# A fused two-block transformer kernel: the second half of the first block spread over more gathers, sums of four gathered loads from the third tile on, norms and branches tile by tile, first gathers issued earlier

## What is computed

```python
# first block
x = x + concat([delta_rule(...) , multiscale_pool(...)]) @ w_out          # "front" work
x = x + _peer(_rmsnorm(x, norm_ffn_w), w_query, sub_keys, expert_down, expert_up)
x = _rmsnorm(x, norm_final_w)
# _peer: 8 heads x 16 experts for each token, out of 16384
q = xb @ w_query ; scores = q . sub_keys ; top_k(16) twice, then top_k(16) of 256 sums
act = gelu(einsum("td,thkd->thk", xb, expert_down[idx]))
out = einsum("thk,thkd->td", gate * act, expert_up[idx])
# second block (c_2, ada_w_2 give shifts, scales, gates)
h = modulate(rms_norm(x, g0), sh_m, sc_m);  y = stick_breaking_mixer(h, w_qkv, w_o)
x = x + gt_m * rms_norm(y, g1)
h = modulate(rms_norm(x, g2), sh_f, sc_f);  y = swiglu_ffn(h, w_in, w_out)
x = x + gt_f * rms_norm(y, g3)
```

## Time and profile before

| what | value |
|---|---|
| median of 3 runs (lowest, highest) | 2576.68 us (2569.09, 2582.97) |
| the profiled execution | 2573.54 us, span of its instructions 2571.7 us, mean granted clock 0.879 |
| busy in the span | PE 1975.4 us (77%), DVE 1311.2, POOL 959.4, ACT 859.8 |
| moved by DMA | 672.54 MB, of it 536.90 MB in the gather queue |
| front list ahead of the loop | up to about 255 us |
| gather loop, first dot to last | 261.4 to 1801.3 us |
| second block | from 1803 us on |

### The profile page before, as it was taken

One profiled execution on the slowest core, in us unless ns is written; L12 is line 12 of the kernel. 1 busy time (PEld: TensorE's weight loads), 2 busy tenths in 40 slices (PEclk: granted clock), 3 DMA queues, 4 the chain that ended last, 5 costly groups with the idle time before them and its releaser, 6 DMA issues.

```text
span 2571.7 us, 24837 instructions
## 1 busy us (share of the span) xinstructions
PE 1975.4 (77%) x8704; PEld 1153.5 (45%) x8704; DVE 1311.2 (51%) x2810; ACT 859.8 (33%) x2260; POOL 959.4 (37%) x725
## 2 busy tenths in 40 slices
PE   8897778878788868765556565555698996999996
PEld 7765555435334235311001110000487665888785
DVE  4523547677775554565667666765401542333301
ACT  3112233334343333333333333332423653222212
POOL 1200323356553333444454445544342002444342
PEclk9999888879799889888776787877799998999998
DMA  6112979989989899999999999999021001222221
GB/s 240 36 58 74 405 290 361 383 330 411 392 334 386 331 373 355 375 417 419 420 420 418 420 379 420 420 420 403 33 99 66 1 1 66 98 92 92 78 99 49
DMA packets 100668, 672.54 MB, mean 262 GB/s; under 512 B 11328, under 2 KB 11328, under 8 KB 31552
## 3 DMA queue, kind: packets, MB, share of 16 engines
q0 software_dynamic: 73728, 536.90, 51.7%
q1 hardware_dynamic: 26816, 134.06, 13.6%
HBM read 668.82 MB, written 2.10 MB: 261 GB/s over the span
## 4 chain that ended last, share of the span: by engine, by line
PE 56%; DMA 19%; DVE 8%; issue 6%; ACT 6%; POOL 5%; SPq 0%; DVEq 0%; POOLq 0%; ACTq 0%; PEldq 0%
PE ps L695 55%; DMA arena<-in_experts,arena_u 16%; POOL arena L1515 4%; DVE arena L1816 3%; DMA gtrow<-in_w_ada 1%; ACT arena L1310 1%; DMA arena<-in_w_ada 1%; ACT sel L1306 1%; ACT L1163 1%; PE ps L706 0%; DMA arena<-in_prow 0%; ACT arena L1169 0%; ACT arena L660 0%; ACT L1306 0%; DVE arena L1882 0%
## 5 line engine op out<-in xcount | busy, mean ns | idle before, releaser
L695 PE MATMUL ps<-arena 128*32 128x512 f32 (+4 forms) x4376 | 1125.3, 553 | 377.1 <-ACT arena L1310 362.7
L695 PEld LDWEIGHTS ps<-arena 128*128 128x128 f32 (+1 forms) x4376 | 493.1, 163 | 949.4 <-ACT arena L1310 539.8
L1515 POOL DMA_INDIRECT arena<-in_experts,arena_u x512 | 599.4, 1171 | 846.7 <-PE ps L695 757.5
L1816 DVE CUSTOM_DVE_ANT_0 arena<-arena 128x1024 f32<-128x1024 f32 x512 | 649.3, 1273 | 386.2 <-DMA arena<-in_experts,arena_u 374.6
L695 PE MATMUL ps<-r_low 128*128 128x512 f32 x1824 | 419.5, 392 | 9.7 <-DVE r_low L1844 7.6
L1538 POOL TENSOR_TENSOR r_low<-middle,r_low 128x1024 fp32r<-128x1024 f32 x98 | 235.6, 2404 | 512.7 <-ACT r_low L1349 512.7
L695 PEld LDWEIGHTS ps<-r_low 128*128 128x128 f32 x1824 | 343.3, 189 | 85.3 <-DVE r_low L1844 6.8
L1306 ACT ACTIVATE sel<-sel 128x1 f32<-128x1 f32 x512 | 102.3, 200 | 648.1 <-DVE sel L1816 647.2
L1349 ACT ACTIVATE r_low<-middle 128x1024 fp32r<-128x1024 f32 x98 | 103.6, 1058 | 281.4 <-PE ps L695 281.3
L1310 ACT ACTIVATE arena<-arena,sel 128x32 f32<-128x32 f32 x512 | 164.5, 321 | 17.2 <-ACT sel L1306 0.5
L695 PE MATMUL ps<-arena,consts 128*32 128x32 f32 (+2 forms) x544 | 75.0, 446 | 96.5 <-POOL arena L1498 69.4
(11 more groups left out here) (201 smaller groups left out, 1518.9 us busy)
## 6 DMA issues: line engine op xcount, KB each, us to landing
middle<-in_w_late SPq DMA_DIRECT2D x24, 2048.0 KB, 7.4
arena<-in_w_front SPq DMA_DIRECT2D x88, 512.0 KB, 7.7
gtrow<-in_w_ada SPq DMA_DIRECT2D x32, 512.0 KB, 8.3
arena<-in_experts,arena_u POOLq DMA_INDIRECT x512, 12.1
arena<-in_w_ada SPq DMA_DIRECT2D x16, 512.0 KB, 9.0
x<-in_x SPq DMA_DIRECT2D x4, 512.0 KB, 9.0
arena<-in_sub_keys SPq DMA_DIRECT2D x2, 1024.0 KB, 10.4
arena<-in_rows SPq DMA_DIRECT2D x4, 512.0 KB, 10.3
```

The costliest lines, as they stand in the source:

```text
L695: return nc.tensor.matmul(out_, lhsT, rhs, start=start, stop=stop_, skip_group_check=skip)
L1515: nc.gpsimd.indirect_dma_start(ring[n % RING], None, a["experts"], bass.IndirectOffsetOnAxis(ap=idxq[:, i % 4, k:k + 1], axis=0),).then_in ...
L1816: nc.vector.tensor_tensor_reduce(r[:, 0:D], r[:, 0:D], xrep[k % 4], 1.0, 0.0, ALU.mult, ALU.add, dots[:, n % 8:n % 8 + 1]).then_inc(s["dot ...
```

## The change

- **Pacing.** Beside the loop more loads are put between stages: projections `p` of half 1 with odd number 3 in place of 2, `u` of half 1 (six levels for each of two chunks) 3 in place of 2, queries `q` of half 1 4 in place of 2, queries 8 to 15 of half 0 3 in place of 2. By walking the two lists, the positions of half 1 are:

| stage | before | after |
|---|---|---|
| queries 8 to 15 of half 0 | 4 to 18 | 5 to 26 |
| n0, tr0 | 19, 22 | 27, 30 |
| p 0 to 11 | 25 to 57 | 33 to 71 |
| kt to i0 of chunk 2 | 70 to 75 | 84 to 89 |
| levels of chunk 2 | 77 to 99 | 91 to 119 |
| kt to i0 of chunk 3 | 113 to 118 | 133 to 138 |
| levels of chunk 3 | 120 to 142 | 140 to 167 |
| pz to om | 152 to 170 | 178 to 196 |
| wo to tr1 | 172 to 192 | 198 to 218 |
| q 0 to 15 | 193 to 224 | 219 to 278 |
| gp, gs (gates) | 228 to 277 | 282 to 331 |

- **Group.** From load 256 on `sums` takes four loads at a time; all four slots are freed together.
- **First loads.** POOL issues loads 0 to 7 right behind its stage `sel 0`, so ahead of the decode for head 1.
- **Tiles 0 to 2 in the loop.** Their final norm, second norm, transposes and modulated copies are done beside loads 337 to 345, 353 to 361 and 433 to 441. The scaling before the transpose is gone: PE multiplies x by a diagonal of the reciprocals (`tdiag`).
- **Seams.** Tile 3 alone is left for seam 1; ACT makes the `a_hi` copies in place of DVE; statistics, branches and the output DMA go tile by tile.

```diff
-        add("p", u, 2 if u else 3)
+        add("p", u, 3 if u == 0 or h == 1 and u % 2 == 1 else 2)
...
-                add("u", (c, lv), 2)
+                add("u", (c, lv), 2 + h)
...
-        add("q", j, 2)
+        add("q", j, 4 if h == 1 else 3 if j > 7 else 2)
...
+        def beside(n, lag):
+
+            gates = STAGES[-1][0]
+            return {gates + 6 + lag: 0, gates + 22 + lag: 1, gates + 102 + lag: 2}.get(n)
...
-            sp.wait_ge(s["fin"], T)
-            sp.dma_start(out.rearrange("b (t p) d -> p (b t) d", p=P), x[:, :, :]).then_inc(s["out"], 16)
+                sp.wait_ge(s["fin"], t + 1)
+                sp.dma_start(out.rearrange("b (t p) d -> p (b t) d", p=P)[:, t, :], x[:, t, :]).then_inc(s["out"], 16)
...
+            def group(n):
+
+                return GROUP if n < 2 * TOPK * PH else 2 * GROUP
...
-                    for k in range(n - GROUP + 1, n + 1):
+                    for k in range(n - group(n) + 1, n + 1):
                         j = k % 4
                         ins = mm(ps[32 * j:32 * j + 32, 6 + h, :], diag[:, m % 4, 32 * j:32 * j + 32],
                                  ring[k % RING][:, D + h * HALF:D + (h + 1) * HALF], False, m % (4 * PH) == 4 * PH - 1, True)
-                ins.then_inc(s["slot_done"], GROUP)
+                ins.then_inc(s["slot_done"], group(n))
...
+            def tile_transposes(t):
+
+                pe.wait_ge(s["xs"], t + 1)
...
+                for kd in range(KD):
+                    ins = mm(ps[:, 1 + kd // 4, kd % 4 * P:(kd % 4 + 1) * P], x[:, t, kd * P:(kd + 1) * P], tdiag[:, t, :])
+                ins.then_inc(s["tr"], 1)
...
-            pe.wait_ge(s["acc_out"], T)
-            pe_transposes(pe, 0, xs2)
+            tile_transposes(T - 1)
...
             pe.wait_ge(s["yfree"], T)
-            pe_transposes(pe, 1, xs2)
+            for t in range(T):
+                pe.wait_ge(s["xs"], T + t + 1)
+                for kd in range(KD):
+                    ins = mm(ps[:, kd, t * P:(t + 1) * P], x[:, t, kd * P:(kd + 1) * P], tdiag[:, t, :])
+                ins.then_inc(s["tr"], 1)
...
+            def tile_stats(t, n):
...
+                nc.scalar.activation(junk, x[:, t, :], ACT.Square, accum_out=stat[:, 0, t:t + 1]).then_inc(s["ssq"], 1)
+                sc.wait_ge(s["ssq"], 2 * t + n + 1)
+                nc.scalar.activation(stat[:, 1, t:t + 1], stat[:, 0, t:t + 1], ACT.Sqrt, bias=EPS, scale=1.0 / D).then_inc(s["sd"], 1)
...
+                if beside(n, 0) is not None:
+                    tile_stats(beside(n, 0), 0)
+                if beside(n, 4) is not None:
+                    tile_stats(beside(n, 4), 1)
+                if beside(n, 8) is not None:
+                    tile_modulate(beside(n, 8))
...
+            tile_stats(T - 1, 0)
...
+            def high(k, kd):
+
+                sc.wait_ge(s["a_y"], KD * T + kd + 1 if k == 1 else KD * T)
+                nc.scalar.activation(a_hi[:, kd, :], y_hT[:, kd, :], ACT.Copy).then_inc(s["a_hi"], 1)
+
+            sc.wait_ge(s["slot_done"], LOADS)
             split(0)
+            tile_stats(T - 1, 1)
             split(1)
-            evac_y(0)
+            tile_modulate(T - 1)
+            for kd in range(KD):
+                high(0, kd)
...
+            for t in range(T + 1):
+                if t < T:
+                    branch(0, t)
+                if t >= 1:
+                    stats_after(t - 1)
+            sc.wait_ge(s["tr"], 2 * T)
+            for kd in range(KD):
+                nc.scalar.activation(y_hT[:, kd, :], ps[:, kd, :], ACT.Identity, bias=modc[:, 2, kd:kd + 1],
+                                     scale=stat_mod(1, kd)).then_inc(s["a_y"], 1)
+                high(1, kd)
...
+                    if stage == "sel" and arg == 0:
+                        for n in range(RING):
+                            load(n)
...
-            for n in range(RING):
-                load(n)
...
+            def tile_norm(t, n):
+
+                ve.wait_ge(s["sd"], 2 * t + n + 1)
+                own.step(nc.vector.reciprocal(stat[:, 1, t:t + 1], stat[:, 1, t:t + 1]))
+                if n == 0:
...
+                    stt(x[:, t, :], x[:, t, :], stat[:, 1, t:t + 1], prow_fin, ALU.mult, ALU.mult).then_inc(s["seln"], 1)
+                else:
+                    ts(tdiag[:, t, :], ident, stat[:, 1, t:t + 1], None, ALU.mult).then_inc(s["xs"], 1)
...
+                    if beside(n, 3) is not None:
+                        tile_norm(beside(n, 3), 0)
+                    if beside(n, 7) is not None:
+                        tile_norm(beside(n, 7), 1)
...
                 for kd in range(KD):
-                    ve.wait_ge(s["a_y"], KD * k + kd + 1)
-                    nc.vector.tensor_copy(a_hi[:, kd, :], y_hT[:, kd, :]).then_inc(s["a_hi"], 1)
                     ve.wait_ge(s["a_hi"], KD * k + kd + 1)
                     tt(a_lo[:, kd, :], y_hT[:, kd, :], a_hi[:, kd, :], ALU.subtract).then_inc(s["a_lo"], 1)
```

More of the change, by code:

```diff
@@ L512, in block_kernel @@
         prow_fin = region(112, D)
-        junk = region(130, D)
+        junk = region(140, D)
+        tdiag = region3(160, T, P)
         qz = region3(80, AH, S)
@@ L981, in sums @@
                 t = m // (4 * PH)
-                if n % (TOPK * PH) == GROUP - 1:
+                if n % (TOPK * PH) == group(n) - 1:
                     if t > 0:
@@ L1016, in _ @@
                     permute(i + 1, t + 1)
-                if n % GROUP == GROUP - 1:
+                if n % group(n) == group(n) - 1:
                     sums(n)
@@ L1024, in _ @@
                 front.upto(n)
+                if beside(n, 8) is not None:
+                    tile_transposes(beside(n, 8))
             def split_tile(out_, u, k, rows_hi, rows_lo):
@@ L1435, in _ @@
                 split(u)
-            branch(1)
+            for t in range(T):
+                branch(1, t)
         @block.gpsimd
@@ L1875, in _, with branch, norm_after @@
             out_lo(AH // 2 - 1)
[L1877 to L1890 removed]
+            def branch(k, t):
+                ve.wait_ge(s["ysq"], 2 * (T * k + t + 1))
+                own.step(nc.vector.reciprocal(stat[:, 3, t:t + 1], stat[:, 3, t:t + 1]))
+                y = ps[:, 2 * t:2 * t + 2, :].rearrange("p b n -> p (b n)")
+                own.step(stt(tail[:, t % 2, :], y, stat[:, 3, t:t + 1], gtrow[:, k, :], ALU.mult, ALU.mult))
+                tt(x[:, t, :], x[:, t, :], tail[:, t % 2, :], ALU.add).then_inc(s["yfree" if k == 0 else "fin"], 1)
+            def norm_after(t):
+                ve.wait_ge(s["sd"], 2 * T + t + 1)
+                own.step(nc.vector.reciprocal(stat[:, 1, t:t + 1], stat[:, 1, t:t + 1]))
+                ts(tdiag[:, t, :], ident, stat[:, 1, t:t + 1], None, ALU.mult).then_inc(s["xs"], 1)
+            for t in range(T + 1):
+                if t < T:
+                    branch(0, t)
+                if t >= 1:
+                    norm_after(t - 1)
             split_hT(1)
@@ L1896, in _ @@
                 tt(act_lo[:, j, :], ff[:, j % 2, :], act_hi[:, j, :], ALU.subtract).then_inc(s["ffd"], 1)
-            ve.wait_ge(s["y"], 2 * T)
-            branch(1)
+            for t in range(T):
+                branch(1, t)
 def laid_out(inputs):
```

103 lines of the change are left out of this document (42 added, 61 removed).

## The result

The changed kernel is **slower by 1.2%**: 2605.62 us (median of 7 runs, 2591.67 to 2613.87) against 2574.67 us before (7 runs), ratio 1.0117 with a 95% interval of 1.0089 to 1.0146. Forecast was 2513 us (2480 to 2550). The profiled execution took 2598.41 us, span 2596.6 us, mean granted clock 0.843 (0.879 before).

A forecast was written before the change was run, and what follows sets the result against it. Gather DMA, ceiling 420 GB/s, was taken to bound the loop, with 115 of 1540 us lost; outside it mostly TensorE. Terms -41 - 12 + 8 + 2 - 15 + 2 - 7 = -63 from 2573.5, median 3.1 higher: 2513 us, range 2480 to 2550.

The forecast's parts named there:

- Sums of four: Loop from load 256: release path of 7.9 to 9.5 us fits 9.96 us of cover; +8 us, bounds 0 to +45.
- Rival 2: Sums from load 256: four groups do not run together, so fours starve the gathers; +99, 2604 us, chance 6%.
- Pacing: Loop beside front stages: spreading projections, levels and queries recovers lost DMA time; -41 us, bounds -15 to -58.
- Queries: Half 1's queries in the loop: 30 more loads recover 22 of the 24.1 us lost there.
- Levels: Chunk 3's levels move behind load 128, away from the turn: 10 us won, plus 1 for chunk 2.
- Projections: Projections in the loop: 9 added loads at 0.85 us each win 8 of the 16.3 us lost.
- Rival 1: Loop: idle DMA time is latency between engines, so spreading gives 10 in place of 41; 2544 us, chance 10%.
- First loads: Loop start: issuing eight loads earlier gives a head start of 15.3 us; -12 us, bounds 0 and -15.
- Tiles in the loop: Work of tiles 0 to 2 beside the loop is hidden but for tenths; +2 us, up to +18.
- seam 1: Between last sum and late matmuls: one tile's work, 13.6 to 15 us for 29.4; -15 us, bounds -18 and -11.
- rival 3: Six statistics in the loop: table switches cost more than their load; +13 us, 2526 us, chance 6%.
- Rivals 4 and 5: Whole kernel: more is won, 2480 to 2490 us, 12%; or the change does less, 2545 to 2565 us, 6%.

The follow-up runs named there:

- e2: Kernel before with four-load sums from load 256 on and nothing else; 2622.8 us, ratio 1.020.
- e5: e2 plus idle identity products on TensorE between the sums from load 288 on, to keep its clock up; 2623.3 us, ratio 1.021.
- e8: e4 with the queries of half 1 at four loads each; 2527.9 us, ratio 0.984 to the kernel before.
- e11: e4 with chunk 3 started 17 loads later, queries of half 1 at three loads and half 1's projections spread; 2586.5 us, ratio 1.007 to the kernel before.
- e12: e8 with chunk 3 and all stages behind it one load later; 2572.9 us, ratio 1.001 to the kernel before.
- e7: Kernel before with only the early issue of loads 0 to 7; 2565.0 us, ratio 0.998.
- e4: Changed kernel with sums of pairs throughout and the old pacing; 2548.8 us, ratio 0.990 to the kernel before.
- e1: Changed kernel with sums of pairs throughout, all else as changed; 2557.4 us, ratio 0.994 to the kernel before.
- e9: Kernel before, pairs throughout, mostly at most six loads in flight from load 288 on; 2626.5 us, ratio 1.020.
- e6: Kernel before, sums in pairs, but slots freed four at a time from load 256 on; 2623.3 us, ratio 1.019.

## Why the prediction was wrong, point by point

- **Sums of four, +8 (bounds 0 to +45): wrong, +48.** With the pacing this is the step that turned the sign: 40 us of the 93 between 2513 and 2606 are here, 48 in the pacing. The failed sentence is "Sum 7.9 to 9.5, so it fits by 0.5 to 2.1 us". Two of its terms were taken from the wrong place. From landing to first issue it had 4.6 to 6.2 us; the cycle above shows 5.8, and the mean in e2 is 6.8. From issue to first data it had 3.3, from load 0, which went out when the core moved almost nothing else; in steady work the first load of a group lands 7.5 us after its issue, 5.0 without its own 2.49. 6.8 + 5.0 = 11.8 against 9.96, where the forecast had at most 9.5.
- **The slack was priced, its slope was not.** The forecast found the path 0.5 us inside its cover and charged only the groups with `soft`. With a path whose own rows differ by 2 us from group to group, a fit of 0.5 us is none. It also charged a shortfall at each of 64 groups; the ring's account has it once in a round of two groups, 32 times.
- **Rival 2 (6%, 2604) had the test, but not the mechanism, and its time is luck.** It added +99 for the fours to -41 for the pacing, 58 in all; measured are +48 and +7, 55. It wanted groups that do not run together, sums of 5.5 us. They run together: 16 instructions in 1.92 us at the high clock, 3.64 at the low one. What took the path past 9.96 was mostly the time from issue to data. The point from which it decides was named rightly, and its chance was far too small for a path computed at 9.5.
- **The clock.** Nearly all sums of four far behind the front's work take about 3.6 us, with 7 to 8 us of idle time ahead of them in the mean. The Trainium skill's "TensorE: Matmul & The Clock Gate" (Part 1: The HAM clock gate) has an idle array fall back to 1.2 GHz, and the trace agrees: 3.64 us in place of 1.92, at granted clocks of 0.58 to 0.67. The forecast's upper 9.5 us had this in it. e5 shows that a warm array alone does not bring the time back; what the low clock adds stays open, as said above.
- **Pacing, -41: wrong, +7 (0 to +13).** Queries: right as a mechanism and nearly in size where they stand free of a turn, -16 to -21 for -22 (e8); in the change they ran to 278, across the turn at 256, and four-load sums. Levels: those of chunk 3 do run at 400 GB/s now, as foretold; but what took their place at the turn, the last steps of chunk 2 and the first of chunk 3, loses 24.1 us in 12 loads, where the forecast's whole stretch of 24 loads around the turn had lost 17.2. The failed step is "chunk 3's levels move behind load 128, away from the turn": it asked what moves away, and not what moves in. Projections, -8: 364 GB/s for 372, and e11 finds 0 to 5. Two counts in this step were also off: by the table of positions the projections get six loads more, not 9 (6 x 0.85 = 5), and the queries 28, not 30.
- **"Loads put between stages cost nothing in sum" left out the place in the pair.** One load is worth 45 us (e12). Neither forecast nor rivals had it.
- **Rival 1 (latency, not crowding)** is half right: the stretches with n0 and tr0, chunk 2's start and the norms kept their loss (16.0, 12.8, 20.1 for 19.4, 13.8, 18.6), as the forecast said, and the projections' in the changed kernel went the way of rival 1; the queries' did not (e8).
- **First loads, -12: -5 (e7).** Failed step: "The head start is 15.3 us", taken as if the loop started with the loads. The first dot stands on DVE behind the selection for head 1. Only its DMA wait of 5.31 us in the earlier trace rows could go.
- **Tiles in the loop, +2; seam 1, -15; seam 2, +2; end, -7:** 13.5, 0 and 7.6 were gained in the last three, within all bounds. Behind the last dot -20.8 for -20. In the loop, the tiles' work costs about 3 us or less (e4). Twelve table loads of 1.28 us came into it, two for each statistic; rival 3 has nothing to show for itself: at 1854.46 the load again starts 0.01 us after the read-out before it ends.
- **Rivals 4 and 5:** 4 did not come. 5 did in part, by its first loads, but its 2545 to 2565 fits only the kernel without the fours (e1, 2557).

## What to carry to other kernels

In a ring of buffers, count what is still in flight when a release happens, and set it against the whole path from landing to landing, measured in steady work and at its slow end. Freeing slots in coarser steps, to save an engine that has time to spare, spends that cover.

Before spacing work out beside a loop, list what comes to lie on the loop's own heavy places and on which side of its release points each stage now stands. Try a shift by one.

Before moving a transfer forward, look at what its first reader waits for: here the gain was no more than the 5.31 us of DMA wait in that reader's row.

## What the runs showed that was not expected

- A shift of some stages by one load out of 512, with not one instruction more or less, moved the time by 45 us (e8 to e12).
- Holding back two of eight slots in 196 of 512 loads cost 57 us (e9): here the gather queue needs more than six loads of 1 MB in flight.
- No gather of 1 MB landed in under 5.35 us from its issue (the least, in e6), though the DMA moves 1 MB in 2.49 us.
- A warmer TensorE (0.88 for 0.60) bought nothing where the DMA was short of slots and the work that kept it warm stood ahead of the sums (e5).
